# First two weight pairs of a hybrid HGRN2 and pooling block: four kinds of sums on GpSimd, masks sooner, splits and transposes in another order

## The chip, the core and the metric

The kernel runs on one core of one Trainium2 chip. The metric is the device time of one launch in microseconds (us). PE is TensorE (its matmuls), DVE is VectorE, ACT is ScalarE, POOL is GpSimd, SP is the queue that loads weights and tokens. L12 is line 12 of the kernel.

## The reference, cut to what matters

```
z = concat(16 meta tokens, x)                 # 1040 x 1024
h = rms_norm(z)                               # x * rsqrt(mean(x*x) + eps) * w
p = h @ w_in + b_in                           # 1024 x 8192: q, f, v, g_hg, u, g_pool, m_hg, m_pool
o = hgrn2_chunkwise(q, k, v, log f)           # 8 heads, chunks of 128 here
y_hg   = (rms_norm(o) * silu(g_hg)) @ w_down_hg
y_pool = (pool(u) @ pool_w * scale * silu(g_pool)) @ w_down_pool
z = z + (sigmoid(m_hg) * y_hg + sigmoid(m_pool) * y_pool) @ w_out
out = rms_norm(z)[16:]
```

All of it is float32. Nearly all of the time goes into the three large products with weights.

## The kernel before, in words

**Products.** Output columns are taken in 40 pairs of 128-column blocks. Each pair is a two by two block product with the 1024 tokens, made with seven smaller products instead of eight. `product(p, i)` is product i of pair p: weights `operand(p, i)` (128 x 512) against one of seven token operands, `R_B11, R_B21, R_V6, R_V5, R_V7, R_B22, R_V4` (i from 0 to 6, 128 x 2048 each). The weights of i = 2 to 5 are sums of the blocks of the raw weights: S2, S1, S3, S4. The token operands of i = 2, 3, 4, 6 are sums of blocks of h: V5 = B11 - B12, V6 = -(B22 + V5), V7 = B22 - B12, V4 = -(V6 + B21).

**Splits.** Each operand is split in a high part (reduced precision, made by ACT: `high(o)` for weights, `first_tile`, `second_tile`, `v5_high`, `v6_high`, `v7_high`, `v4_high` for tokens) and a low part, the exact operand less the high one (made by DVE: `low(o)`, `b22_low`, `v5_low` and so on). A product is 12 matmuls of 128 columns by 512: high by high, high by low and low by high for four blocks. Weight number o in `ORDER` uses slot o % 4 of a ring, so `high(o)` waits for product o - 4. In this order the first 14 products are (0,0) (0,1) (1,0) (1,1) (0,5) (1,5) (0,3) (1,3) (0,2) (1,2) (0,4) (1,4) (0,6) (1,6). They are called o0 to o13 below, and (2,0) is o14.

**Start.** x comes in eight tiles of 128 rows. For tile i ACT squares it (`square_x`), DVE makes the mean (`x_mean`), POOL the inverse root by pow (L556), DVE the row of h (`h_row`), PE turns it (`h_transposes`), and ACT and DVE copy and split it out of PSUM (`first_tile` and `first_low` for tiles 1 to 4, `second_tile` and `b22_low` for 5 to 8). o0 needs the low parts of tiles 1 to 4 (semaphore `h_lo` at 4), o4 all eight tiles, o6 `v5_lo`, o8 `v6_lo`, o10 `v7_lo`, o12 `v4_lo`.

**Orders.** Each engine runs a list that is written out by hand. DVE's list up to o14 holds, beside the splits, the weight sums of pairs 0 and 1 (`early_sums`, L1530 to L1534, and `early_third_sum`, L1539: eight of 128x512), the sums V5, V6, V7 and V4 (`v7_sum` L1472 and `v4_sum` L1505: two halves of 128x1024 each) and the sums of products that leave PSUM (`add_11`, `add_12`, `add_22`, `early_fifth`). POOL makes the inverse roots and then, when the last is made, the masks of the recurrence (memset L560, selects L563 and L579, casts L585 and L586), which DVE and ACT need before `prepare(0)`, just ahead of o14. The SP queue sends the weights of pair 2 when the low part of o12 is made (L475).

After o14 pairs follow one another, with the recurrence of the head before woven between products.

Of the kernel before, what the change touches and what calls it, by code (L numbers as in the profile page):

```python
# [12 lines left out]
P = 128  # L13
# [140 lines left out]
def hybrid_block(nc, x, meta, norm_w, wstream, pool_w, b_in, lb_logits, hg_norm_w, pool_scale, final_norm_w, out):  # L154
    names = ExitStack()
    with names:
# [7 lines left out]
            "hm_cleared", "hm_copied",  # L164
# [370 lines left out]
        def _(pool):  # L535
# [24 lines left out]
            steps.mark(pool.memset(mask1[:, :, :], 1.0))  # L560

            def keep(mask, base, channel, pattern):
# [3 lines left out]
            level0 = mask1[:, 0:2, :].rearrange("p a (b j) -> p (a b) j", j=2)  # L566
            odd = mask1[:, 3, :]
            halves = [(m, mask1[:, n, :].rearrange("p (b j) -> p b j", j=1 << m), lo, hi)
                      for m, n, lo, hi in ((1, 2, 0, 1), (2, 4, 0, 3), (3, 5, 4, 7), (3, 6, 0, 3), (4, 7, 0, 15))]
# [3 lines left out]
            for m, view, lo, _ in halves:  # L573
                keep(view, -lo, 1, [[-(2 << m), 64 >> m], [0, 1 << m]])
# [3 lines left out]
            for m, view, _, hi in halves:  # L578
                steps.mark(pool.affine_select(out=view, in_=view, compare_op=ALU.is_ge, fill=0.0, base=hi,  # L579
                                              pattern=[[2 << m, 64 >> m], [0, 1 << m]], channel_multiplier=-1))  # L580
            steps.settle()
            whole = mask1[:, 0:2, :].rearrange("p a t -> p (a t)")
            for g in range(GROUPS):
                rows = slice(g * GROUP, (g + 1) * GROUP)
                pool.tensor_copy(mask[rows, 0, :], whole[rows, rows])  # L585
                ins = pool.tensor_copy(mask[rows, 2:MASKS, 0:16], mask1[rows, 2:MASKS, g * 16:(g + 1) * 16])  # L586
            ins.then_inc(S["masks_spread"], 1)
# [76 lines left out]
        def _(act):  # L664
# [64 lines left out]
            def v4_high(n):  # L729
                c = slice(n * 2 * P, (n + 1) * 2 * P)  # L730
                act.wait_ge(S["v4_made"], n + 1)
                act.activation(r_hi[R_V4][:, :, c], r_lo_f[R_V4][:, :, c], ACT.Copy).then_inc(S["v4_hi"], 1)
# [222 lines left out]
            first_tile(4)  # L955
            square_x(6)
            high(1)
            square_x(7)
            act.wait_ge(S["lb_shifted"], 1)
            act.activation(lexp[:, :, :], lexp[:, :, :], ACT.Exp).then_inc(S["lb_exp"], 1)  # L960
            square_x(8)
            high(2)
# [6 lines left out]
            meta_copy(0, 0)  # L969
            second_tile(8)  # L970
            high(4)
            copy_first(1)
            v5_high()
            high(5)
            act.activation(o_ms[:, 0:1], minus_half[:, 0:1], ACT.Sigmoid)
            copy_early_fifth(0)
            high(6)
# [11 lines left out]
            meta_copy(0, 1)  # L989
            copy_second(1)  # L990
            v4_high(0)
            v4_high(1)
            high(11)
            act.wait_ge(S["lb_made"], 1)
            gates(0)
            high(12)
            high(13)
            prepare_copies(0)
            last_quarter(0)
            high(14)  # L1000
            high(15)
# [142 lines left out]
        def _(pe):  # L1144
# [92 lines left out]
            def product(p, i):  # L1237
                half(p, i, 0)
                half(p, i, 1)
# [184 lines left out]
        def _(dve):  # L1424
# [21 lines left out]
            def first_low(i):  # L1446
                c = slice((i - 1) * P, i * P)
                lower, upper = banks_of(i)
                dve.wait_ge(S["h_hi"], i)
                dve.tensor_tensor(r_lo[R_B11][:, :, c], lower, r_hi[R_B11][:, :, c].bitcast(F32), ALU.subtract)  # L1450
                dve.tensor_copy(b11_whole[:, :, c], lower)
# [14 lines left out]

            def v7_sum(n):

                dve.wait_ge(S["h_copied"], CHUNKS)
                dve.wait_ge(S["v6_made"], n + 1)  # L1470
                b22 = r_lo_f[R_V7][:, :, two(n)]
                dve.tensor_tensor(b22, b22, b12_whole[:, :, two(n)], ALU.subtract).then_inc(S["v7_made"], 1)  # L1472
# [30 lines left out]
            def v4_sum(n):  # L1503
                dve.wait_ge(S["v6_made"], n + 1)
                dve.scalar_tensor_tensor(r_lo_f[R_V4][:, :, two(n)], v6_whole[:, :, two(n)], -1.0, r_lo_f[R_V4][:, :, two(n)],  # L1505
                                         ALU.mult, ALU.subtract).then_inc(S["v4_made"], 1)

# [11 lines left out]
            def early_sums(p):  # L1519

                dve.wait_ge(raw_loaded[2 * p], 16)
                if p:
                    dve.wait_ge(S["early_loaded"], 16)
                    dve.wait_ge(S["h_row"], 8)
                else:
                    dve.wait_ge(raw_loaded[1], 16)
                a11, a12 = raw_half(p, 0, 0), raw_half(p, 0, 1)
                a21, a22 = (raw_early[:, 0:HALF], raw_early[:, HALF:D]) if p else (raw_half(0, 1, 0), raw_half(0, 1, 1))
                made, done = (sums_early if p else sums), S["sums_made"]
                dve.tensor_tensor(made[S1][:, :], a21, a22, ALU.add).then_inc(done, 1)  # L1530
                dve.wait_ge(done, sum_made(p, S1))
                dve.tensor_tensor(made[S2][:, :], made[S1][:, :], a11, ALU.add).then_inc(done, 1)
                dve.wait_ge(done, sum_made(p, S2))
                dve.tensor_tensor(made[S4][:, :], made[S2][:, :], a12, ALU.add).then_inc(done, 1)  # L1534

            def early_third_sum(p):

                a21 = raw_early[:, 0:HALF] if p else raw_half(0, 1, 0)
                dve.tensor_tensor((sums_early if p else sums)[S3][:, :], raw_half(p, 0, 0), a21, ALU.add) \  # L1539
                    .then_inc(S["sums_made"], 1)  # L1540

            def weight_sums(p):
# [4 lines left out]
                done = S["sums_made"]  # L1547
                dve.wait_ge(S["w_lo"], (POS[0, 4] if p == EARLY else POS[p - 1, 5]) + 1)
# [262 lines left out]
            first_low(1)  # L1811
            h_row(3)
            x_mean(4)
            first_low(2)
            h_row(4)
            x_mean(5)
            first_low(3)
            low(0)
            first_low(4)
            h_row(5)  # L1820
            x_mean(6)
            low(1)
            h_row(6)
            x_mean(7)
            low(2)
            h_row(7)
            x_mean(8)
# [4 lines left out]
            v5_sum(6)  # L1832
            add_11(0)
            low(3)
            early_sums(0)
            b22_low(7)
            v5_sum(7)
            b22_low(8)
            v5_sum(8)
            low(4)  # L1840
            early_sums(1)
            low(5)
            v5_low()
            add_11(1)
            low(6)
            dve.wait_ge(S["lb_exp"], 1)
# [7 lines left out]
            v6_sum(0)  # L1854
            v6_sum(1)
            low(7)
            v6_low(0)
            v6_low(1)
            early_fifth(0)
            low(8)  # L1860
            low(9)
            v7_sum(0)
            v7_sum(1)
            early_third_sum(0)
            early_third_sum(1)
            v7_low(0)
            v7_low(1)
            low(10)
            v4_sum(0)
            v4_sum(1)  # L1870
            add_12(0)
            low(11)
            add_22(0)
            v4_low(0)
            v4_low(1)
            low(12)
# [3 lines left out]
            add_22(1)  # L1880
            dve.wait_ge(S["masks_spread"], 1)
            prepare(0)
            low(14)
# [412 lines left out]
```

## Time and profile before

| | us |
|---|---|
| median of three runs (1080.66 to 1082.76) | 1081.52 |
| the profiled execution, its own time | 1081.81 |
| its span | 1079.9 |
| PE busy | 1040.1 (96%) |
| DVE busy | 778.2 (72%) |
| ACT busy | 490.4 (45%) |
| POOL busy | 97.7 (9%) |

The profiled execution took 1.9 us more than its span, for what lies around it. Busy times are shares of the span over very unlike stages: they say which engine is nearly full, not what a change in the first 80 us is worth. A start and a duration are read together: two instructions of one engine overlap by some 0.08 us, so that a DVE instruction of 0.68 us follows the one before at 0.60.

### The profile page before, as it was taken

The numbers are of one execution on the slowest core, as the hardware profiler recorded it, in microseconds if no ns is written. First come the engines' busy times: TensorE is split into PE (matmuls) and PEld (weight loads), VectorE is DVE, ScalarE is ACT, GpSimd is POOL, SyncE is SP. The second block draws the span as 40 slices with busy tenths as digits, with TensorE's granted clock in tenths as the row PEclk, the third lists the DMA queues.
The fourth block names the chain that finished last, engine by engine and source line by source line (L and its number), as shares of the span: only waits on it lengthen the run. The fifth ranks groups of instructions, "written<-read, shape, count | busy, mean of one in ns | idle before, by whom it ended". The sixth has DMA issues, their size and how long they took to land. (4 is left out here: it accounts for less than half of the span.)

```text
span 1079.9 us, 18838 instructions
## 1 busy us (share of the span) xinstructions
PE 1040.1 (96%) x7444; PEld 844.6 (78%) x7444; DVE 778.2 (72%) x1245; ACT 490.4 (45%) x841; POOL 97.7 (9%) x164
## 2 busy tenths in 40 slices
PE   7879999999999999999999999999999999999995
PEld 6657888888888888787888787788887787787884
DVE  7887686868686868686676767774569789978233
ACT  7664535353545454443353533344457246245122
POOL 2500010101010101010101010001110110000111
PEclk9999999999999999999999999999999999999998
DMA  6022020202020111122212121227332674555232
GB/s 257 1 81 77 21 80 21 80 20 80 21 70 31 61 39 60 41 69 79 80 57 89 58 89 50 82 74 301 117 108 98 236 271 156 175 177 175 69 121 103
DMA packets 36055, 104.61 MB, mean 97 GB/s; under 512 B 4576, under 2 KB 4576, under 8 KB 35968
## 3 DMA queue, kind: packets, MB, share of 16 engines
q1 hardware_dynamic: 22064, 65.61, 18.6%
q0 software_dynamic: 8240, 26.79, 6.7%
q10 hardware_dynamic: 5664, 11.02, 2.7%
q8 instruction: 59, 0.97, 0.4%
q14 instruction: 28, 0.23, 0.1%
HBM read 78.23 MB, written 25.17 MB: 96 GB/s over the span
## 5 line engine op out<-in xcount | busy, mean ns | idle before, releaser
L1149 PE MATMUL acc<-r_hi,w_hi 128*128 128x512 f32 x1112 | 448.0, 403 | 15.3 <-DVE w_lo L1516 5.3
L1149 PE MATMUL acc<-r_hi,w_lo 128*128 128x512 f32 x1112 | 434.2, 390 | 0.0
L1149 PE MATMUL acc<-r_lo,w_hi 128*128 128x512 f32 x1112 | 433.9, 390 | 0.0
L1149 PEld LDWEIGHTS acc<-r_hi,w_hi 128*128 128x128 f32 x1112 | 208.8, 188 | 70.4 <-issue 22.9
L1149 PEld LDWEIGHTS acc<-r_hi,w_lo 128*128 128x128 f32 x1112 | 208.7, 188 | 45.0
L1149 PEld LDWEIGHTS acc<-r_lo,w_hi 128*128 128x128 f32 x1112 | 209.1, 188 | 39.0
L678 ACT ACTIVATE w_hi<-sum 128x512 fp32r<-128x512 f32 x156 | 97.9, 628 | 150.5 <-DVE sum L1552 81.7
L1516 DVE TENSOR_TENSOR w_lo<-sum,w_hi 128x512 fp32r<-128x512 f32 x156 | 106.5, 686 | 59.8 <-ACT w_hi L678 59.5
L1516 DVE TENSOR_TENSOR w_lo<-raw,w_hi 128x512 fp32r<-128x512 f32 x120 | 82.1, 687 | 68.1 <-ACT w_hi L678 68.0
L678 ACT ACTIVATE w_hi<-raw 128x512 fp32r<-128x512 f32 x120 | 74.6, 624 | 26.2 <-PE acc L1149 26.2
L1149 PE MATMUL acc<-wo_hi,m_hi 128*128 128x512 f32 x128 | 49.9, 390 | 0.6 <-DVE wo_lo L2187 0.6
L1149 PE MATMUL acc<-wo_lo,m_hi 128*128 128x512 f32 x128 | 49.8, 389 | 0.0
L1149 PE MATMUL acc<-wo_hi,m_lo 128*128 128x512 f32 x128 | 49.8, 389 | 0.0
L762 ACT ACTIVATE second<-acc,bias 128x512 f32<-128x512 f32 x31 | 21.2, 685 | 61.0 <-PE acc L1149 60.9
L591 POOL TENSOR_TENSOR o_rs<-o_ms,minus_half 128x8 f32<-128x8 f32 x8 | 16.0, 2004 | 328.9 <-DVE o_ms L1769 328.9
L762 ACT ACTIVATE fifth<-acc,bias 128x512 f32<-128x512 f32 x31 | 21.3, 687 | 44.7 <-PE acc L1149 44.6
L762 ACT ACTIVATE first<-acc,bias 128x512 f32<-128x512 f32 x32 | 22.1, 690 | 38.0 <-PE acc L1149 37.9
L2051 DVE TENSOR_TENSOR r_lo<-stage,r_hi 128x2048 fp32r<-128x2048 f32 x14 | 32.0, 2285 | 1.9 <-ACT r_hi L1068 1.9
L1149 PEld LDWEIGHTS acc<-wo_hi,m_hi 128*128 128x128 f32 x128 | 24.0, 188 | 6.1 <-DVE wo_lo L2187 1.1
L1320 PE MATMUL miscs<-st,qx 128*128 128x128 f32 x128 | 25.6, 281 | 2.7 <-DVE st L1758 2.7
L1149 PEld LDWEIGHTS acc<-wo_hi,m_lo 128*128 128x128 f32 x128 | 24.0, 188 | 5.0
L1149 PEld LDWEIGHTS acc<-wo_lo,m_hi 128*128 128x128 f32 x128 | 24.0, 188 | 4.8
(287 smaller groups left out, 1380.5 us busy)
## 6 DMA issues: line engine op xcount, KB each, us to landing
raw<-in_wstream SPq DMA_DIRECT2D x88, 512.0 KB, 3.7
xin<-in_x SPq DMA_DIRECT2D x8, 512.0 KB, 6.1
a_spill<-gt POOLq DMA_DIRECT2D x16, 256.0 KB, 4.0
c_spill<-pg POOLq DMA_DIRECT2D x16, 256.0 KB, 2.7
stage<-a_spill ACTq DMA_DIRECT2D x4, 1024.0 KB, 12.4
smh_spill<-zq POOLq DMA_DIRECT2D x16, 256.0 KB, 2.6
gate_in<-smh_spill SPq DMA_DIRECT2D x16, 256.0 KB, 4.8
part_spill<-zq POOLq DMA_DIRECT2D x16, 256.0 KB, 4.7
```

Of the source, the lines that this page charges most:

```text
L591: pool.tensor_tensor(o_rs[:, :], o_ms[:, :], minus_half[:, 0:CHUNKS], ALU.pow).then_inc(S["o_rstd"], 1)
L678: act.activation(w_hi[o % RING][:, :], operand(o), ACT.Copy).then_inc(S["w_hi"], 1)
L762: return act.activation(dst, src, ACT.Identity, bias=b, scale=scale)
L1149: ins = pe.matmul(out_ap, a, b, start=first and n == 0, stop=final and n == 2, skip_group_check=partial)
L1320: pe.matmul(dst, qt[:, s], st[:, s], start=True, stop=False)
L1516: dve.tensor_tensor(w_lo[o % RING][:, :], operand(o), w_hi[o % RING][:, :].bitcast(F32), ALU.subtract) \
L2051: dve.tensor_tensor(r_lo[i][:, :, :], STAGED[i][:, :, :], r_hi[i][:, :, :].bitcast(F32), ALU.subtract) \
```

## The change

It touches the stage before o14 alone.

- POOL makes the eight weight sums of pairs 0 and 1 and the sums V7 and V4, which DVE made. V4 was one instruction of the form (in0 * -1) - in1; ACT now keeps B21 with its sign turned (`scale=-1.0`), so that V4 is a plain subtraction, -B21 - V6.
- POOL's mask instructions are put between the inverse roots, and the casts that spread the masks behind the weight sums.
- `first_low` is cut in three (`b11_low`, `b11_copy`, `b21_low`), and o0 waits only for the four low parts of B11.
- ACT, PE and DVE run their lists in another order: `high(4)` to `high(15)` sooner, transposes 5 to 8 half a product or more later, the tail of the lower bound's arithmetic (`lb`) later, V6 behind `v5_low` and ahead of `low(7)`.
- The third weight sums come before the masks are spread. `v4_high(n)` waits for `v6_low(n)` too, and `v7_sum` for the masks. `weight_sums(2)` waits for all eight early sums. The second pair's sums wait for all nine rows of h.

```diff
@@ gpsimd
-            for i in range(CHUNKS + 1):
+            def x_rstd(i):
                 rows = META if i == 0 else P
                 pool.wait_ge(S["x_mean"], i + 1)
                 pool.tensor_tensor(x_rs[...], x_ms[...], minus_half[...], ALU.pow).then_inc(S["x_rstd"], 1)
...
+            def early_sum(p, s):
...
+                if s == S1:
+                    pool.wait_ge(raw_loaded[2 * p], 16)
+                    if p:
+                        pool.wait_ge(S["early_loaded"], 16)
+                        pool.wait_ge(S["h_row"], CHUNKS + 1)
+                    else:
+                        pool.wait_ge(raw_loaded[1], 16)
+                    a, b = a21, a22
...
+                pool.tensor_tensor(made[s][:, :], a, b, ALU.add).then_inc(done, 1)
+            def v7_sum(n):
...
+                pool.wait_ge(S["h_copied"], CHUNKS)
+                pool.wait_ge(S["h_lo"], CHUNKS)
+                pool.wait_ge(S["v6_made"], n + 1)
+                pool.wait_ge(S["masks_spread"], 1)
+                b22 = r_lo_f[R_V7][:, :, c]
+                pool.tensor_tensor(b22, b22, b12_whole[:, :, c], ALU.subtract).then_inc(S["v7_made"], 1)
+            def v4_sum(n):
...
+                pool.wait_ge(S["v6_made"], n + 1)
+                b21 = r_lo_f[R_V4][:, :, c]
+                pool.tensor_tensor(b21, b21, v6_whole[:, :, c], ALU.subtract).then_inc(S["v4_made"], 1)
+            x_rstd(0)
+            steps.mark(pool.memset(mask1[:, :, :], 1.0))
+            (2 selects) x_rstd(1) (2) x_rstd(2) (2) x_rstd(3) (3) x_rstd(4) (2) x_rstd(5) (3) x_rstd(6)
+            early_sum(0, S1)
+            x_rstd(7)
+            early_sum(0, S2)
+            x_rstd(8)
+            early_sum(0, S4)
+            early_sum(1, S1)
+            early_sum(1, S2)
+            early_sum(1, S4)
+            early_sum(0, S3)
+            early_sum(1, S3)
+            spread_masks()
+            v7_sum(0)
+            v7_sum(1)
+            v4_sum(0)
+            v4_sum(1)
@@ scalar
-                act.activation(r_lo_f[R_V4][:, :, c], upper, ACT.Copy).then_inc(S["h_copied"], 1)
+                act.activation(r_lo_f[R_V4][:, :, c], upper, ACT.Copy, scale=-1.0).then_inc(S["h_copied"], 1)
...
             v6_high(0)
             v6_high(1)
-            high(7)
             high(8)
             high(9)
             v7_high(0)
+            high(10)
+            copy_second(0)
             v7_high(1)
-            copy_second(0)
-            high(10)
+            high(11)
@@ tensor
-                if p == 0 and i < 2:
+                if p == 0 and i == 0:
+                    pe.wait_ge(S["b11_lo"], 4)
+                elif p == 0 and i == 1:
                     pe.wait_ge(S["h_lo"], 4)
...
             product(0, 0)
+            half(0, 1, 0)
             h_transposes(5)
-            half(0, 1, 0)
+            half(0, 1, 1)
             h_transposes(6)
-            half(0, 1, 1)
+            half(1, 0, 0)
             h_transposes(7)
-            product(1, 0)
+            half(1, 0, 1)
             h_transposes(8)
@@ vector (the new order from tile 3 on)
+            h_row(4) x_mean(5) b11_low(3) low(0) b11_copy(3) b11_low(4) b21_low(3) b11_copy(4) b21_low(4) low(1)
+            h_row(5) x_mean(6) x_mean(7) h_row(6) x_mean(8) low(2) h_row(7) b22_low(5) v5_sum(5) h_row(8) b22_low(6)
+            add_11(0) low(3) v5_sum(6) b22_low(7) v5_sum(7) b22_low(8) low(4) v5_sum(8) low(5) add_11(1) low(6) v5_low()
+            v6_sum(0) v6_sum(1) low(7) v6_low(0) low(8) v6_low(1) early_fifth(0) low(9) (lb) v7_low(0) low(10) v7_low(1)
+            low(11) add_12(0) v4_low(0) add_22(0) low(12) v4_low(1) early_fifth(1) add_12(1) low(13) add_22(1) low(14)
+            prepare(0) low(15) weight_sums(2) low(16)
```

The lists of POOL's selects and of DVE are written in one line each here; in the kernel each call has its own line.

## Rows read from the trace of the kernel before

**Rows 1.** The page, parts 1 and 2: busy time; TensorE's granted clock in 40 slices.

```profile
PE 1040.1 (96%) x7444; PEld 844.6 (78%) x7444; DVE 778.2 (72%) x1245; ACT 490.4 (45%) x841; POOL 97.7 (9%) x164
PEclk9999999999999999999999999999999999999998
```

**Rows 2.** Busy time by stretch: start:end, length, PE, PEld, DVE, ACT, POOL, clock, DMA.

```profile
30.00:40.00 10.00, 9.02 (x50) 7.32 (x48) 9.93 (x15) 7.05 (x15) 9.79 (x17) 1.00 0.00 1
60.00:70.00 10.00, 7.10 (x32) 5.29 (x31) 8.96 (x11) 7.86 (x13) 0.00 (x0) 1.00 0.17 52
23.44:79.20 55.76, 46.24 (x237) 35.19 (x237) 47.25 (x64) 36.88 (x58) 15.15 (x26) 1.00 0.12 38
79.20:127.00 47.80, 47.59 (x530) 37.64 (x530) 34.92 (x70) 22.72 (x43) 1.16 (x2) 1.00 0.17 57
127.00:1065.00 938.00, 926.38 (x6547) 753.51 (x6548) 676.33 (x1078) 412.26 (x706) 73.57 (x113) 1.00 0.29 98
```

**Rows 3.** Timeline of PE: start, duration, instruction, idle before and its releaser.

```profile
20.02 1.50 PE L1335 MATMUL acc<-ident 128*128 128x128 f32 x12
23.44 0.47 PE L1149 MATMUL acc<-r_hi,w_hi 128*128 128x512 f32 x1 [1.91 <-DVE r_lo L1453]
...
40.46 0.47 PE L1149 MATMUL acc<-r_hi,w_hi 128*128 128x512 f32 x1 [1.44 <-DVE w_lo L1516]
...
43.07 0.39 PE L1149 MATMUL acc<-r_hi,w_lo 128*128 128x512 f32 x1
...
79.20 0.47 PE L1149 MATMUL acc<-r_hi,w_hi 128*128 128x512 f32 x1 [0.92 <-DVE w_lo L1516]
```

**Rows 4.** Timeline of DVE: splits of tile 4, sums that move, one that stays.

```profile
21.41 0.68 DVE L1450 TENSOR_TENSOR r_lo<-miscs,r_hi 128x512 fp32r<-128x512 f32 x1
22.01 0.68 DVE L1451 COPY b_whole<-miscs 128x512 f32<-128x512 f32 x1
22.61 0.68 DVE L1453 TENSOR_TENSOR r_lo<-miscs,r_hi 128x512 fp32r<-128x512 f32 x1
...
56.64 2.36 DVE L1472 TENSOR_TENSOR r_lo_f<-r_lo_f,b_whole 128x1024 f32<-128x1024 f32 x2
...
62.99 2.35 DVE L1505 SCALAR_TENSOR_TENSOR r_lo_f<-b_whole,r_lo_f 128x1024 f32<-128x1024 f32 x2
```

**Rows 5.** Groups of POOL's instructions by form: count, busy, mean ns.

```profile
L542 POOL TENSOR_SCALAR_AFFINE_SELECT stack<-stack 128x16 f32<-128x16 f32 x4 | 0.8, 199 | 0.7 <-POOL stack L539 0.2
L560 POOL MEMSET mask<- 128x512 f32 x1 | 0.5, 526 | 0.0
L545 POOL TENSOR_SCALAR_AFFINE_SELECT ident<-ident 128x128 f32<-128x128 f32 x1 | 0.3, 294 | 0.1
L537 POOL MEMSET ident<- 128x128 f32 x1 | 0.2, 205 | 0.3 <-POOLq L2286 0.3
```

**Rows 6.** Timeline of POOL: the masks.

```profile
30.74 5.79 POOL L563 TENSOR_SCALAR_AFFINE_SELECT mask<-mask 128x128 f32<-128x128 f32 x9
36.48 3.36 POOL L579 TENSOR_SCALAR_AFFINE_SELECT mask<-mask 128x64 f32<-128x64 f32 x5
```

**Rows 7.** Timeline of DVE before, and beside, POOL's selects.

```profile
28.21 1.29 DVE L1440 SCALAR_TENSOR_TENSOR hrow<-xin,x_rs,nw 128x1024 f32<-128x1024 f32 x1 [0.67 <-PE levels L1251]
...
30.96 1.47 DVE L1440 SCALAR_TENSOR_TENSOR hrow<-xin,x_rs,nw 128x1024 f32<-128x1024 f32 x1
...
32.36 0.72 DVE L1483 TENSOR_TENSOR r_lo<-r_lo_f,r_hi 128x512 fp32r<-128x512 f32 x1
...
35.61 0.82 DVE L1532 TENSOR_TENSOR sum<-sum,raw 128x512 f32<-128x512 f32 x1
...
39.64 0.72 DVE L1516 TENSOR_TENSOR w_lo<-sum,w_hi 128x512 fp32r<-128x512 f32 x1
```

**Rows 8.** Timelines of POOL and DVE around 139 us.

```profile
138.24 2.06 POOL L591 TENSOR_TENSOR o_rs<-o_ms,minus_half 128x8 f32<-128x8 f32 x1 [54.69 <-DVE o_ms L1769]
```

```profile
138.68 0.70 DVE L1689 TENSOR_TENSOR kt<-kt,fg 128x520 f32<-128x520 f32 x1
```

More of the change, by code:

```diff
@@ L557, in _, with runs @@
                                    ALU.pow).then_inc(S["x_rstd"], 1)
-            steps.mark(pool.memset(mask1[:, :, :], 1.0))
+            level0 = mask1[:, 0:2, :].rearrange("p a (b j) -> p (a b) j", j=2)
+            odd = mask1[:, 3, :]
+            def runs(m, n):
+                return mask1[:, n, :].rearrange("p (b j) -> p b j", j=1 << m)
             def keep(mask, base, channel, pattern):
@@ L564, in keep, with keep_from @@
                                               pattern=pattern, channel_multiplier=channel))
[L566 to L569, printed above, removed]
+            def keep_from(m, n, lo):
+                keep(runs(m, n), -lo, 1, [[-(2 << m), 64 >> m], [0, 1 << m]])
@@ new lines, in keep_to, with spread_masks @@
+            def keep_to(m, n, hi):
+                keep(runs(m, n), hi, -1, [[2 << m, 64 >> m], [0, 1 << m]])
+            def spread_masks():
+                steps.settle()
+                pool.wait_ge(S["sums_made"], 4 * EARLY)
+                whole = mask1[:, 0:2, :].rearrange("p a t -> p (a t)")
+                for g in range(GROUPS):
+                    rows = slice(g * GROUP, (g + 1) * GROUP)
+                    pool.tensor_copy(mask[rows, 0, :], whole[rows, rows])
+                    ins = pool.tensor_copy(mask[rows, 2:MASKS, 0:16], mask1[rows, 2:MASKS, g * 16:(g + 1) * 16])
+                ins.then_inc(S["masks_spread"], 1)
@@ new lines, in early_sum @@
+            def early_sum(p, s):
+                a11, a12 = raw_half(p, 0, 0), raw_half(p, 0, 1)
+                a21, a22 = (raw_early[:, 0:HALF], raw_early[:, HALF:D]) if p else (raw_half(0, 1, 0), raw_half(0, 1, 1))
+                made, done = (sums_early if p else sums), S["sums_made"]
+                if s == S1:
[6 more added lines that the diff above has]
+                    a, b = a21, a22
+                elif s == S2:
+                    pool.wait_ge(done, sum_made(p, S1))
+                    a, b = made[S1][:, :], a11
+                elif s == S4:
+                    pool.wait_ge(done, sum_made(p, S2))
+                    a, b = made[S2][:, :], a12
+                else:
+                    a, b = a11, a21
+                pool.tensor_tensor(made[s][:, :], a, b, ALU.add).then_inc(done, 1)
@@ L572, in _ @@
             keep(odd, -1, 1, [[-2, 64]])
-            for m, view, lo, _ in halves:
-                keep(view, -lo, 1, [[-(2 << m), 64 >> m], [0, 1 << m]])
+            x_rstd(1)
+            keep_from(1, 2, 0)
+            keep_from(2, 4, 0)
+            x_rstd(2)
+            keep_from(3, 5, 4)
+            keep_from(3, 6, 0)
+            x_rstd(3)
+            keep_from(4, 7, 0)
             steps.settle()
@@ L577, in _ @@
             keep(odd, 1, -1, [[2, 64]])
[L578 to L587, printed above, removed]
+            x_rstd(4)
+            keep_to(1, 2, 1)
+            keep_to(2, 4, 3)
+            x_rstd(5)
+            keep_to(3, 5, 7)
+            keep_to(3, 6, 3)
+            keep_to(4, 7, 15)
+            x_rstd(6)
+            early_sum(0, S1)
[13 more added lines that the diff above has]
+            v4_sum(1)
             def o_rstd(r):
@@ L969, in _ @@
             meta_copy(0, 0)
+            high(4)
             second_tile(8)
-            high(4)
+            high(5)
             copy_first(1)
+            high(6)
             v5_high()
-            high(5)
             act.activation(o_ms[:, 0:1], minus_half[:, 0:1], ACT.Sigmoid)
             copy_early_fifth(0)
-            high(6)
+            high(7)
             copy_early_fifth(1)
@@ L1517, in low @@
                     .then_inc(S["w_lo"], 1)
[L1519 to L1540, printed above, removed]
             def weight_sums(p):
@@ L1810, in _ @@
             x_mean(3)
-            first_low(1)
+            b11_low(1)
+            b11_copy(1)
+            b21_low(1)
             h_row(3)
             x_mean(4)
-            first_low(2)
+            b11_low(2)
+            b11_copy(2)
+            b21_low(2)
             h_row(4)
             x_mean(5)
-            first_low(3)
+            b11_low(3)
             low(0)
-            first_low(4)
+            b11_copy(3)
+            b11_low(4)
+            b21_low(3)
+            b11_copy(4)
+            b21_low(4)
+            low(1)
             h_row(5)
             x_mean(6)
-            low(1)
+            x_mean(7)
             h_row(6)
-            x_mean(7)
+            x_mean(8)
             low(2)
             h_row(7)
-            x_mean(8)
             b22_low(5)
@@ L1838, in _ @@
             b22_low(8)
+            low(4)
             v5_sum(8)
-            low(4)
-            early_sums(1)
             low(5)
-            v5_low()
             add_11(1)
             low(6)
+            v5_low()
+            v6_sum(0)
+            v6_sum(1)
+            low(7)
+            v6_low(0)
+            low(8)
+            v6_low(1)
+            early_fifth(0)
+            low(9)
             dve.wait_ge(S["lb_exp"], 1)
@@ L1853, in _ @@
             dve.tensor_scalar(one_minus_lb[:, :], lb[:, :], -1.0, 1.0, ALU.mult, ALU.add).then_inc(S["lb_made"], 1)
[L1854 to L1865, printed above, removed]
             v7_low(0)
+            low(10)
             v7_low(1)
-            low(10)
-            v4_sum(0)
-            v4_sum(1)
+            low(11)
             add_12(0)
-            low(11)
+            v4_low(0)
             add_22(0)
-            v4_low(0)
+            low(12)
             v4_low(1)
-            low(12)
             early_fifth(1)
@@ L1880, in _ @@
             add_22(1)
+            low(14)
             dve.wait_ge(S["masks_spread"], 1)
             prepare(0)
-            low(14)
             low(15)
```

48 lines of the change are left out of this document (24 added, 24 removed).

## The prediction

> **What bounds the kernel now.** I read the page first. PE is busy 96% of the span, and its clock is the higher of its two levels, 2.4 GHz, in every slice but the last [rows 1]. So a gain has to be found where PE is not busy. The busy times by stretch say where that is. From 79.20 to 127 us PE idles 0.2 of 47.8 us, and up to 1065 us it idles 11.6 of 938 us, spread thinly. From 23.44 us, when o0 starts, to 79.20 us, when o14 starts, it idles 55.76 - 46.24 = 9.5 us, 17% [rows 2]. Behind o14 PE's own work sets the pace, so a time at which o14 starts sooner or later comes through to the end one for one. The start of o14 is the number to predict.
>
> The timeline of PE names the waits. o0 begins 1.9 us after the last warming matmul, released by DVE's low part of tile 4 (L1453). Nine breaks follow, the first ahead of o4 (1.44 us) and the last ahead of o14 (0.92 us), most of them released by `low` (L1516) on DVE [rows 3]. PE's ends are modelled. The twelve starts of o4 lie 0.24 us apart, but its last matmul is shown as 0.39 long, so each break is some 0.16 longer from start to start. Nine of these make 1.5 us, and the true idle time is 11.0 us. DVE itself is busy 9.93 of 10 us from 30 to 40, and 8.96 from 60 to 70 [rows 2]. It is the engine behind these waits.
>
> **The change part by part.**
>
> o0's wait. It now waits for `b11_low(4)`. Before, DVE did B11 low, the copy and B21 low of tile 4 one after another, 21.41 to 23.29 [rows 4]. In the new list `b11_low(4)` starts when ACT has made the high part, 20.8, and ends at 21.5, as PE's warming matmuls do. o0 starts at 21.5: 1.9 us gained, if nothing later takes it back.
>
> What leaves DVE. Eight sums at 0.60 us are 4.8, V7 and V4 at 2.28 each from start to next start [rows 4] are 4.6. Together 9.4 us.
>
> With DVE never hindered, I walked the four lists, each instruction starting when its engine is free and its semaphores stand, with the spacings of these timelines (0.60 for 512 columns on DVE, 1.14 for 1024, 0.49 and 1.05 on ACT, 1.41 for half a product). The same walk over the old lists gives o14 at 78.6, against 79.20 in the trace. The new lists give o4 37.0, o8 49.0, o10 55.2, o12 60.9 and o14 68.0. Breaks of 0.4 and 0.5 us are left, and 1.4 ahead of o14, where ACT's `high(14)` stands behind the four gate instructions. That is 10.6 us sooner: 1.9 + 11.0 - 2.3. The order of splits and transposes has no price of its own in it. The transposes that slip cost nothing because o1 to o3 stand between them, and the later `lb` nothing because ACT's gates come 11 us after it; were either cover gone, 0.8 us for a transposition or 0.7 us for `lb` would show. Pair 2's weights leave SP when the low part of o12 stands, which is sooner by as much, so they keep their distance. New waits: behind `v7_sum` on POOL stands `v4_sum`, and for it ACT's `v4_high`. Behind ACT's `copy_second(0)` (o8's end) stands `v7_high(1)`, and DVE's `v7_low(1)` waits for that 2 us in the walk, under cover of o8 and o9.
>
> What comes to POOL. No row shows a plain sum there. A memset of 512 columns took 0.526 and one of 128 took 0.205; a select of 128 columns took 0.294 and of 16 took 0.199 [rows 5]. Both give 0.84 us per thousand columns over a floor near 0.19. A sum reads two operands; if they go one after the other a 512-column sum takes 0.19 + 0.87 = 1.06 and a 1024-column one 1.93. Twelve sums are 8 x 1.06 + 4 x 1.93 = 16.2 us. From the seventh inverse root (25.7) POOL has time: unhindered, V7 begins at 43 and V4's second half at 49, ready for o10 (55) and o12 (61). The inverse roots for tiles 7 and 8 now stand behind a sum each. That sets `h_row(7)` back by at most 1.1 us, covered by o1 and o2.
>
> What the two do to each other. This decides. While POOL ran its masks, 14 selects took 9.1 us, 0.65 each, for a kind that takes some 0.25 alone [rows 5, 6]: each waited for the DVE instruction in hand. DVE lost little, but it lost something at each one. An `h_row` took 1.47 instead of 1.29, a sum 0.82, eight others, from 32.36 to 39.64, 0.72 instead of 0.685 [rows 7]. All these read two operands from SBUF. Together DVE lost 0.60 us while the selects read 2 x 128 + 12 x 64 = 1024 columns: 0.60 us per thousand. The moved sums read 8 x 1024 + 4 x 2048 = 16384 columns. At that rate they hold DVE for 9.8 us. Of DVE's 30.7 us from `h_row(7)` to `low(13)` only eight instructions (4.8 us: `add_11`, `add_12`, `add_22`, `early_fifth`, one operand from PSUM) are of another kind, so I let 0.8 of it fall on the path: 7.8 us.
>
> The Trainium skill (SBUF — State Buffer, "Who interferes with whom") has the same as a rule: a VectorE instruction with two SBUF inputs and a GpSimd instruction that reads SBUF use one read interface, and the later one is blocked until the first has finished. The rows bear out the waiting on both sides. By the duration that GPSIMD Engine Reference, "Performance versus the Vector engine", states for a sum of 2048 columns (4497 ns), an estimate for the twelve sums is 17.2 us of hold, and the sum below would be 1084.7 instead.
>
> **The sum.** 10.6 - 7.8 = 2.8 us sooner. The profiled execution took 1081.81, 1.9 more than its span, and would take 1079.0; the median of runs lies 0.3 lower: 1078.7.
>
> Bounds of the hold. Below: nothing, 10.6 sooner, 1070.9. A 520-column product of DVE beside a POOL pow of 2.06 us took 0.70, no longer than elsewhere [rows 8], so a POOL instruction doesn't hold DVE by its mere presence. Above, from the 128-column selects alone: 0.18 us lost beside one [rows 7] is 1.4 us per thousand columns, and 23 us of hold, 18 on the path, 7.8 slower. I take 0.60 because it comes from all 14, and halfway between the two rates, 1.0, for the far end of the range: 16.4 x 0.8 = 13.1, 2.5 slower, 1084.0; some 1.5 us of error of the walk on top, 1085.5. The walk shows why this end is near. With POOL's V7 and V4 sums each holding DVE 1.7 us, they fall between `v6_sum(1)`, `low(7)`, `v6_low(0)`, `low(8)` and `v6_low(1)`, and o8 waits nearly 6 us.
>
> **Rivals.**
>
> *A. DVE is held for the whole of each POOL sum.* The twelve sums last 16.2 us; 13.0 on the path: 2.4 slower, 1083.9. From 1082.0, if the fixed 0.19 us of each is free (13.9 us of hold), to 1085.5, if a sum is slower than 1.06 us. It turns the change into a loss from a hold of 13.3 us on, 0.81 per thousand columns. For it: the loss beside 128-column selects. Against it: the loss beside those of 64 columns, 0.035, less than 64 columns take at POOL's pace (0.054).
>
> *B. DVE is hardly held.* POOL's reads fit into gaps, or run ahead. 1071 to 1074.5. For it: the pow row and the small mean loss. Against it: all selects were delayed by DVE, so the two do exclude each other.
>
> *C. POOL becomes the bound.* If a sum of 1024 columns takes 4 us, V4 is complete at 43 + 16 = 59 and its two high and two low parts at 63, and o12 waits 2 us beyond the rest: 1073 when nothing is held, 1081 with the hold of my sum. It needs a rate four times that of the rows.
>
> **Chances.** Forecast case (1075 to 1081.2) 0.39; A 0.36; B 0.19; C and others 0.06. A reaches from 1081.2 to 1086. By what a measurement of this kernel can tell from no change, 0.2% or 2.2 us, faster means below 1079.4: B, two thirds of the forecast case, 0.47 in all. Within 0.2%: the rest of the forecast case and a quarter of A, 0.23. Slower, over 1083.7: 0.30. The range 1070.9 to 1085.5 leaves 0.12 out, mostly above. The likeliest case alone spans 1075 to 1081.2.
>
> **What the next profile would show.** o0 at 21.5 (right if within 0.3). POOL's sums at 1.06 and 1.93, plus up to 0.6 of waiting. DVE's two-operand instructions between 26 and 58 lengthened: by 0.6 for each 512-column sum and 1.2 for each 1024-column one in my case, 1.1 or more in A, none in B. o4 near 40.7, o8 between 53 and 57, o14 near 76. If o14 starts before 71 or after 79, the hold was mis-sized. If it starts as foretold and the end does not follow, the pace behind o14 is not PE's own.

## The result, and the profile after

| | before | after |
|---|---|---|
| median us | 1081.57 (7 runs, 1080.66 to 1082.76) | 1086.08 (7 runs, 1085.23 to 1086.36) |
| the profile's span, us | 1079.9 | 1084.3 |
| start of o0 / o4 / o14, us | 23.44 / 40.46 / 79.20 | 21.30 / 43.90 / 84.49 |

The ratio of after to before is 1.0039, with a 95% interval of 1.0028 to 1.005: the kernel became 4.5 us slower, where 2.8 us sooner was forecast. It arises ahead of o14, which starts 5.3 us later.

The page of the kernel after, parts 1 and 2 (beside [rows 1]): DVE has 6.3 us more busy time, although twelve of its instructions went away, and POOL 24.1 us more.

```profile
PE 1044.0 (96%) x7444; PEld 848.5 (78%) x7444; DVE 784.5 (72%) x1233; ACT 489.6 (45%) x841; POOL 121.8 (11%) x176
PEclk9889999999999999999999999999999999999998
```

The busy times by stretch of the kernel after (beside [rows 2]; start:end, length, PE, PEld, DVE, ACT, POOL, clock, DMA):

```profile
40.00:50.00 10.00, 6.11 (x16) 4.92 (x17) 9.83 (x10) 5.12 (x7) 6.29 (x10) 0.66 0.17 56
...
60.00:70.00 10.00, 6.63 (x17) 5.22 (x18) 6.77 (x9) 1.13 (x2) 2.14 (x1) 0.66 0.00 0
...
21.30:84.49 63.19, 50.69 (x236) 39.37 (x237) 56.71 (x58) 37.98 (x62) 31.36 (x23) 0.89 0.11 35
84.49:1069.00 984.51, 973.34 (x7075) 790.88 (x7076) 709.51 (x1141) 434.71 (x749) 74.54 (x115) 1.00 0.28 96
```

From o0 to o14 PE now needs 63.19 us for what took 55.76, and idles 12.5 of them instead of 9.5. PE's busy time rose too, 50.69 against 46.24, and in two of the stretches its clock is 0.66. The timeline of PE in the kernel after (beside [rows 3]) says where:

```profile
21.30 0.47 PE L1227 MATMUL acc<-r_hi,w_hi 128*128 128x512 f32 x1 [0.17 <-DVE r_lo L1531]
...
36.58 0.47 PE L1227 MATMUL acc<-r_hi,w_hi 128*128 128x512 f32 x1 [1.28 <-DVE w_lo L1593]
...
43.90 0.77 PE L1227 MATMUL acc<-r_hi,w_hi 128*128 128x512 f32 x1 [4.31 <-DVE w_lo L1593]
44.46 0.63 PE L1227 MATMUL acc<-r_lo,w_hi 128*128 128x512 f32 x1
44.88 0.63 PE L1227 MATMUL acc<-r_hi,w_lo 128*128 128x512 f32 x1
...
63.37 0.77 PE L1227 MATMUL acc<-r_hi,w_hi 128*128 128x512 f32 x1 [4.81 <-DVE r_lo L1571]
...
84.49 0.50 PE L1227 MATMUL acc<-r_hi,w_hi 128*128 128x512 f32 x1 [1.15 <-ACT vt L840]
```

o0 starts 2.1 us sooner. The nine breaks became five, 12.5 us in all, two of them large: 4.31 us ahead of o4 and 4.81 ahead of o8, both released by DVE. Behind each the matmuls start 0.43 us apart instead of 0.23: the granted clock is at the lower of its two levels, 1.2 GHz, from 42.3 to 49.1 and from 62.7 to 69.5 us. The timelines of DVE and of POOL in the kernel after, first DVE (beside [rows 4, 7]):

```profile
25.47 2.31 DVE L1521 SCALAR_TENSOR_TENSOR hrow<-xin,x_rs,nw 128x1024 f32<-128x1024 f32 x1 [0.61 <-POOL x_rs L556]
...
31.18 1.77 DVE L1550 TENSOR_TENSOR r_lo_f<-b_whole 128x512 f32<-128x512 f32 x1
...
34.68 0.68 DVE L1656 TENSOR_TENSOR fg<-acc,first 128x512 f32<-128x512 f32 x1
35.28 1.16 DVE L1593 TENSOR_TENSOR w_lo<-raw,w_hi 128x512 fp32r<-128x512 f32 x1
36.36 1.78 DVE L1550 TENSOR_TENSOR r_lo_f<-b_whole 128x512 f32<-128x512 f32 x1
...
50.92 2.90 DVE L1593 TENSOR_TENSOR w_lo<-sum_early,w_hi 128x512 fp32r<-128x512 f32 x1
53.99 3.17 DVE L1571 TENSOR_TENSOR r_lo<-b_whole,r_hi 128x1024 fp32r<-128x1024 f32 x1 [0.17 <-ACT r_hi L795]
57.09 2.86 DVE L1593 TENSOR_TENSOR w_lo<-sum,w_hi 128x512 fp32r<-128x512 f32 x1
59.87 3.36 DVE L1571 TENSOR_TENSOR r_lo<-b_whole,r_hi 128x1024 fp32r<-128x1024 f32 x1
...
70.54 1.23 DVE L1582 TENSOR_TENSOR r_lo<-r_lo_f,r_hi 128x1024 fp32r<-128x1024 f32 x1 [3.66 <-ACT r_hi L804]
```

```profile
25.40 1.29 POOL L607 TENSOR_TENSOR sum<-raw 128x512 f32<-128x512 f32 x1
26.65 1.53 POOL L556 TENSOR_TENSOR x_rs<-x_ms,minus_half 128x1 f32<-128x1 f32 x1
...
34.33 1.56 POOL L607 TENSOR_TENSOR sum_early<-raw_early 128x512 f32<-128x512 f32 x1 [1.92 <-DVE hrow L1521]
...
50.10 5.98 POOL L617 TENSOR_TENSOR r_lo_f<-r_lo_f,b_whole 128x1024 f32<-128x1024 f32 x2 [3.54 <-DVE b_whole L1560]
56.04 6.10 POOL L624 TENSOR_TENSOR r_lo_f<-r_lo_f,b_whole 128x1024 f32<-128x1024 f32 x2
```

POOL's first sum starts at 25.40 and lasts 1.29. The row of h that starts at 25.47 takes 2.31 instead of 1.28: DVE lost 1.03 us. A 512-column difference beside a sum takes 1.77 instead of 0.68. `add_11` at 34.68, with one operand in PSUM, takes its usual 0.68 beside the sum of 34.33, and only the `low` behind it is lengthened, by 0.48, for the rest of that sum. Beside V7 and V4 four DVE instructions take 2.90, 3.17, 2.86 and 3.36 where 0.69 and 1.22 are usual. Added over all twelve sums, DVE was held for 7.95 us by the eight of 512 columns (1.07 for a full one) and for 8.47 us by the four of 1024 (2.1 each): 16.4 us for 16384 columns read, 1.00 us per thousand. What left DVE was 9.4 us. The trade costs DVE 7.0 us. V7 and V4 do worse than their own balance, 8.5 us of hold against 4.6 that left: the hold falls wholly ahead of o8, the saving behind it, where DVE stands 3.66 us for the second high part of V7. ACT makes that behind its copy of o8's result, so it can't come sooner than o8 lets it.

### The profile page after: what moved, and what is told of

Same layout as the page of the kernel before. It is cut to its first block and busy times, and to the rows that moved or that the text cites. A ratio compares the mean times of both kernels' runs of the same rounds, so it can differ in the third digit from the quotient of the medians.

```text
span 1084.3 us, 18844 instructions
## 1 busy us (share of the span) xinstructions
PE 1044.0 (96%) x7444; PEld 848.5 (78%) x7444; DVE 784.5 (72%) x1233; ACT 489.6 (45%) x841; POOL 121.8 (11%) x176
## 5 line engine op out<-in xcount | busy, mean ns | idle before, releaser
L1593 DVE TENSOR_TENSOR w_lo<-sum,w_hi 128x512 fp32r<-128x512 f32 x156 | 108.8, 701 | 60.0 <-ACT w_hi L755 59.7
L704 POOL DMA_DIRECT2D c_spill<-pg x16 | 8.6, 539 | 181.8 <-DVE pg L2054 181.3
```

The lines of the kernel that those rows point to most:

```text
L704: pool.dma_start(c_dram[2 * g + k // 2, k % 2], pg[:, k // 2, (k % 2) * HALF:(k % 2 + 1) * HALF]).then_inc(c_stored[k], 16)
L1593: dve.tensor_tensor(w_lo[o % RING][:, :], operand(o), w_hi[o % RING][:, :].bitcast(F32), ALU.subtract) \
```

## The experiments

Three theories stood after this. **Hold**: DVE stands still while a sum of POOL reads, if DVE's instruction has both operands in SBUF, and this net 7 us is most of the loss. **Order**: the new lists themselves are bad. **Clock**: the lower clock behind the two waits is most of the loss. A fourth, that DVE or PE simply waits for POOL's results, is out by the rows above: V4's second half is ready at 62.1 us, and no break stands ahead of o10 or o12. Every kernel but those said otherwise is the kernel after with the edit shown. Ratios and differences are to the kernel before, which ran again beside each group of them (medians 1082.08, 1082.30 and 1082.10 us).

### All sums on DVE again, everything else of the change kept

```diff
-            early_sum(0, S1)      # POOL: all eight, v7_sum, v4_sum
...
+            early_sums(0)         # DVE: ahead of v5_sum(6)
+            early_sums(1)         # ahead of low(4)
+            v7_sum(0) v7_sum(1) early_third_sum(0) early_third_sum(1) v4_sum(0) v4_sum(1)
```

The masks are then spread behind the last inverse root, without waiting for the sums.

> The changed kernel with its eight weight sums and the sums V7 and V4 put back on DVE; the early start of o0, the masks between the inverse roots and all other orders stay. Theory 1 (DVE is held for some 1.07 us by each 512-column sum of POOL and 2.1 us by each 1024-column one, and this hold makes the loss): nothing holds DVE, o4 near 39, o8 near 53, o14 near 75.5, time 1077.7 (1076 to 1079.5). Theory 2 (the new order of splits, transposes and high parts costs by itself): 1081.5 or more, with waits at the same places as in the changed kernel. Theory 3 (the waits are cheap, the fall of TensorE's clock behind the two long ones makes most of the loss): the clock stays at the higher level, and the time is that of the changed kernel less 5.2 us, 1080.9.

Measured: 1077.09 us (1076.07 to 1077.28), ratio 0.9954, interval 0.994 to 0.9967. This is 5.0 us faster than before and 9 faster than after. The timeline of PE with all sums on DVE:

```profile
38.63 0.47 PE L1215 MATMUL acc<-r_hi,w_hi 128*128 128x512 f32 x1 [2.08 <-DVE w_lo L1581]
...
60.62 0.47 PE L1215 MATMUL acc<-r_hi,w_hi 128*128 128x512 f32 x1 [2.06 <-DVE r_lo L1570]
```

o4 starts 5.3 us sooner than after, with twelve sums more on DVE's list. So the order isn't what costs: the theory of the order fell, and the new order, with the early start and the masks between the inverse roots, is itself a gain. The second wait shown, 2.06 us, stands ahead of o10.

### Only the weight sums, only V7 and V4, only the early start

```diff
 (only the weight sums on POOL: V7 and V4 back)
-            v7_sum(0) v7_sum(1) v4_sum(0) v4_sum(1)          # POOL
+            v7_sum(0) v7_sum(1) ... v4_sum(0) v4_sum(1)      # DVE
 (only V7 and V4 on POOL: weight sums back)
-            early_sum(0, S1) ... early_sum(1, S3)            # POOL
+            early_sums(0) ... early_sums(1) ... early_third_sum(0) early_third_sum(1)   # DVE
 (kernel before with the early start alone)
-                if p == 0 and i < 2:
+                if p == 0 and i == 0:
+                    pe.wait_ge(S["b11_lo"], 4)
...
-            first_low(3)
+            b11_low(3)
...
-            first_low(4)
+            b11_low(4)
+            rest_low(3)
+            rest_low(4)
```

> The changed kernel with V7 and V4 back on DVE; POOL makes the eight weight sums only. Theory 1: DVE loses some 8 us up to o4, which starts near 44 as in the changed kernel; then no more is lost, no long wait ahead of o8, o14 near 77 to 79, time 1079.7 to 1082 (the higher figure if the clock falls behind the wait ahead of o4 and nothing hides it). Theory 2: over 1084. Theory 3: one fall of the clock instead of two, 1083.5.

> The changed kernel with the weight sums back on DVE; POOL makes V7 and V4 only. Theory 1: o4 near 39; DVE loses 8.5 us around v6_low, o8 near 61 with a wait over 4 us ahead of it, the clock falls there, o14 near 80 to 83, time 1082.8 to 1085.7. This part of the change costs more than the weight sums do. Theory 2: 1084 or more, with no more lost at v6_low than elsewhere. Theory 3: one fall of the clock, 1083.5.

> The kernel before with one part of the change: the low part of B11 of tile 4 is made ahead of the other four splits of tiles 3 and 4, and o0 waits for it alone. o0 starts at 21.3 to 21.5 instead of 23.44. If DVE's list sets the time from o4 on, as I think, the rest comes no sooner: wait ahead of o4 grows from 1.4 to 3, o14 near 79, time 1081.5 (1080.5 to 1082). If PE's own work mattered there, 1079.6.

| kernel | median us | ratio, interval | o4 | o14 |
|---|---|---|---|---|
| only the weight sums on POOL | 1080.00 | 0.9984, 0.9976 to 0.9993 | 44.06 | 78.46 |
| only V7 and V4 on POOL | 1084.25 | 1.0021, 1.0012 to 1.003 | 38.55 | 81.53 |
| before, early start alone | 1081.66 | 0.9995, 0.9986 to 1.0004 | 39.83 | 78.58 |

The timeline of PE with only the weight sums on POOL has the wait ahead of o4, while o8 (the second row) starts without one:

```profile
44.06 0.77 PE L1223 MATMUL acc<-r_hi,w_hi 128*128 128x512 f32 x1 [4.33 <-DVE w_lo L1589]
...
58.65 0.39 PE L1223 MATMUL acc<-r_hi,w_hi 128*128 128x512 f32 x1
```

With only V7 and V4 on POOL it is the other way round: o8 waits 6.38 us, and a `low` beside a sum of V7 takes 2.88 us. Timelines of PE and DVE:

```profile
60.97 0.77 PE L1219 MATMUL acc<-r_hi,w_hi 128*128 128x512 f32 x1 [6.38 <-DVE r_lo L1563]
```

```profile
48.58 2.88 DVE L1585 TENSOR_TENSOR w_lo<-sum_early,w_hi 128x512 fp32r<-128x512 f32 x1
```

Each group of sums makes its own wait. Against all sums on DVE (1077.09) the weight sums cost 2.9 us, near the 3.1 by which they hold DVE longer than they save it. V7 and V4 cost 7.2, where that balance is 3.9: their saving comes behind o8, and the clock is at 1.2 GHz from 58.6 to 65.4 us; what each of the two adds was not told apart. Together that is 10.1, where the whole change costs 9.0. The early start alone brings o0 2.6 us forward (23.44 to 20.84) and o14 by 0.6; its 0.4 us at the end can't be told from nothing. PE waits part of it away ahead of o4 (2.46 instead of 1.44 us) and loses part to the clock, which is at 1.2 GHz from 40.8 to 44.2 us. DVE's work is the limit, not the time at which PE begins.

### The kernel after, with PE kept at work in the two waits

```diff
+                if (p, i) in ((0, 5), (0, 2)):
+                    pe.wait_ge(S["h_copied"], CHUNKS - 1)
+                    for _ in range(18 if i == 5 else 20):
+                        pe.matmul(small[:, 0:P], ident[:, :], ident[:, :], start=True, stop=True)
```

> The changed kernel with warming matmuls (128 columns, into a PSUM bank that is free then) on PE: 18 ahead of o4 and 20 ahead of o8, the two waits of 4.3 and 4.8 us behind which the clock was at its lower level for 5.6 and 6.2 us. DVE and POOL are left alone. If the hold of DVE makes most of the loss and the clock the rest, o4 and o8 start as late as before (43.9, 63.4), the products behind o8 take 2.76 us each again, and 2 to 3 us come back: 1083.5 (1082.5 to 1084.5). The first slow stretch gives nothing back, since o8 waits for DVE anyway. If the clock were most of the loss, both stretches would come back: 1080.9.

The extra matmuls write scratch in PSUM that nobody reads. Measured: 1084.53 us (1083.37 to 1087.31), ratio 1.0024, interval 1.0015 to 1.0032, in the timeline of PE:

```profile
39.70 4.18 PE L1446 MATMUL levels<-ident 128*128 128x128 f32 x36
44.20 0.47 PE L1227 MATMUL acc<-r_hi,w_hi 128*128 128x512 f32 x1 [0.32 <-DVE w_lo L1597]
...
63.66 0.47 PE L1227 MATMUL acc<-r_hi,w_hi 128*128 128x512 f32 x1 [1.92 <-DVE r_lo L1575]
```

o4 and o8 start when they did (0.3 later), because DVE sets them, but their matmuls run at the higher level. 1.0039 to 1.0024 is 1.6 us, uncertain by about 1.5, as the two intervals just overlap; 2 to 3 were expected. In the profiled executions o14 starts 2.3 us sooner (82.22) and the span is 1.7 shorter. The clock is a minor part of the loss, and its theory as the main cause fell.

The same trick on the kernel with all sums on DVE (8 matmuls ahead of o4 and o10), where the clock was low from 61.2 to 64.6 us:

> The kernel with all sums on DVE and eight warming matmuls ahead of o4 and of o10, where PE waited 2.1 us each and behind the second of which the clock was at its lower level from 61.4 to 64.6 us. If the clock there costs what its matmuls lost (3.2 us at half rate), 1.5 us come back: 1075.5. If the fall is chance from run to run, the time stays within 0.5 us of 1077.1.

Measured 1077.14 us (1077.07 to 1078.31), ratio 0.9956, interval 0.9944 to 0.9969: no change from 1077.09. In its timeline of PE the time saved is waited away two products later, ahead of o12:

```profile
67.60 0.47 PE L1215 MATMUL acc<-r_hi,w_hi 128*128 128x512 f32 x1 [0.97 <-DVE r_lo L1579]
```

The lower clock cost nothing here because DVE was behind anyway; the expected gain missed for that reason.

### Three kinds of work on POOL beside the same DVE

The kernel before, with four memsets, four copies and four sums of 128x512 added to POOL behind the masks, all on scratch. ACT waits for them before it uses that scratch, so the kernel's time is not compared; its rows are.

```diff
+            left, right = vv[:, 0:HALF], vv[:, HALF:SEQ]
+            for kind in range(3):
+                for n in range(4):
+                    (0) pool.memset((left, right)[n % 2], 0.0)
+                    (1) pool.tensor_copy(left, right)
+                    (2) pool.tensor_tensor(left, left, right, ALU.add)
```

> The kernel before, and behind its masks POOL runs 4 memsets, 4 copies and 4 sums of 128x512 on scratch, one after another, while DVE works through v5_low, V6 and its splits (43 to 60 us). A reading of the hold by kind. If DVE is held for as long as POOL reads, a memset holds nothing, a copy about 0.45 us, a sum 1.07 us. If it is held for the whole instruction, a memset 0.5, a copy 0.6, a sum 1.28. If the hold has to do with POOL's writes, a memset holds DVE too. The time is not the question; some 5 us slower.

Measured: 1086.36 us, one run. The timelines of POOL and DVE; the last of the four copies, and each of the two V6 sums (L1493), are shown by themselves:

```profile
44.13 2.28 POOL L594 MEMSET vv<- 128x512 f32 x4
46.48 3.48 POOL L596 COPY vv<-vv 128x512 f32<-128x512 f32 x4
49.32 0.63 POOL L596 COPY vv<-vv 128x512 f32<-128x512 f32 x1
50.04 7.37 POOL L598 TENSOR_TENSOR vv<-vv 128x512 f32<-128x512 f32 x4
```

```profile
44.63 2.28 DVE L1509 TENSOR_TENSOR r_lo<-r_lo_f,r_hi 128x2048 fp32r<-128x2048 f32 x1
46.83 0.68 DVE L1615 TENSOR_TENSOR qx<-acc,first 128x512 f32<-128x512 f32 x1
47.44 0.68 DVE L1531 TENSOR_TENSOR w_lo<-sum,w_hi 128x512 fp32r<-128x512 f32 x1
48.03 0.57 DVE L1862 TENSOR_TENSOR lmax<-lexp 128x8 f32<-128x8 f32 x1
...
49.40 1.63 DVE L1493 SCALAR_TENSOR_TENSOR b_whole<-r_lo_f,r_lo_f 128x1024 f32<-128x1024 f32 x1
50.95 2.31 DVE L1493 SCALAR_TENSOR_TENSOR b_whole<-r_lo_f,r_lo_f 128x1024 f32<-128x1024 f32 x1
54.91 1.38 DVE L1531 TENSOR_TENSOR w_lo<-sum_early,w_hi 128x512 fp32r<-128x512 f32 x1 [1.64 <-ACT w_hi L691]
56.21 3.42 DVE L1504 TENSOR_TENSOR r_lo<-b_whole,r_hi 128x1024 fp32r<-128x1024 f32 x2
```

Four memsets, which read nothing, ran beside a DVE instruction with two operands in SBUF without lengthening it (2.28, its usual time). A copy, which reads 512 columns, held `lmax`, 8 columns of the lower bound, for 0.42 us (0.57 instead of 0.15), and another held the first V6 sum for 0.42 (1.63 instead of 1.21). A sum, which reads 1024, held the second V6 sum for 1.10 (2.31), and one of the two V6 low parts for 1.06 (3.42 for two that take 2.36). The `low` at 54.91, which began while a sum was under way, was held for the rest of it, 0.69. So what holds DVE is how much POOL reads, and not that POOL is busy.

### All sums on DVE, with DVE's and ACT's lists reordered

```diff
 (ACT)  second_tile(5) behind high(3), high(6) and v6_high(0) sooner, v4_high(0) behind v7_high(0), v7_high(1) ahead of copy_second(0)
 (DVE)  the weight sums one at a time between splits instead of three in a row; low(2) behind add_11(0);
        early_third_sum(0) ahead of low(8), v4_sum ahead of v7_sum, v7_low(0) and v7_low(1) ahead of lb, early_fifth(0) later
```

> The kernel with all sums on DVE (1077.09 in its run), with the lists of DVE and ACT put in an order in which each sum and split comes just ahead of its user: S1 of pair 0 between the rows of h, second_tile(8) ahead of high(4), V7's high parts ahead of copy_second. DVE's work is the same, its idle time less. A walk over the lists gives o14 3.9 us sooner than for the kernel with all sums on DVE: 1073.5 (1072 to 1076). If DVE's plain amount of work sets the time there, nothing comes of it: 1077.

Measured: 1072.88 us (1072.45 to 1073.77), ratio 0.9917, interval 0.9903 to 0.993: 9 us faster than before, the best version here. Its timeline of PE (o4 and o10), and its busy times from 60 to 70 us:

```profile
37.75 0.47 PE L1215 MATMUL acc<-r_hi,w_hi 128*128 128x512 f32 x1 [0.40 <-DVE w_lo L1581]
...
59.17 0.47 PE L1215 MATMUL acc<-r_hi,w_hi 128*128 128x512 f32 x1 [1.39 <-DVE r_lo L1570]
```

```profile
60.00:70.00 10.00, 10.00 (x46) 8.02 (x45) 10.00 (x15) 8.56 (x12) 0.00 (x0) 1.00 0.56 191
```

PE and DVE are both full there, with POOL idle.

### Two sums given back to POOL, in two places

From that best version, S1 and S2 of pair 0 go to POOL again: once at 19 us, where DVE's splits have an operand in PSUM, and once beside the rows of h, whose operands are in SBUF.

```diff
             x_rstd(5)
+            early_sum(0, S1)      # first kernel
+            early_sum(0, S2)
...
             x_rstd(6)
+            early_sum(0, S1)      # second kernel
             x_rstd(7)
+            early_sum(0, S2)
```

> The version with all sums on VectorE and its lists reordered, with the first two weight sums of pair 0 given back to GpSimd, at once behind the reciprocal root of the sixth row tile, so from about 19 us on, where VectorE does splits whose second operand is in PSUM (such a split was not lengthened in the two traces where a sum of GpSimd ran beside it). Theory of the hold (VectorE stands while GpSimd reads, if VectorE has two operands in SBUF): if the raw weights have landed by 22 us both sums lie beside PSUM splits and cost nothing, VectorE's list is 1.2 us shorter, and the time is 1071.7 to 1072.9. If the weights come later, or the reciprocal roots of the next tiles are put back by the sums, the rows of h come later and it is 1073 to 1075. Rival (any work that leaves VectorE helps by its own length, wherever GpSimd does it): about 1072, the same as its neighbour with the sums under the rows of h.

> The same two sums on GpSimd, but one behind the reciprocal root of the seventh and one behind that of the eighth row tile, so beside the rows of h, which have two operands in SBUF. Theory of the hold: each sum lengthens a row of h from 1.28 to about 2.3 us and saves 0.6 us later, so these rows' transposes and the product behind them come 1 to 2 us later and the list is 0.9 us longer in all; 1073.0 to 1074.9. Rival (any work that leaves VectorE helps by its own length): about 1072, like its neighbour.

Measured: 1073.33 us (1072.37 to 1073.56), ratio 0.9919 (0.9905 to 0.9933), for the first place, and 1075.95 us (1074.0 to 1076.55), ratio 0.994 (0.9928 to 0.9953), for the second. The same two sums cost 2.6 us more in the second place. Timelines of POOL and DVE in the first place:

```profile
19.33 1.73 POOL L607 TENSOR_TENSOR sum<-raw 128x512 f32<-128x512 f32 x1
21.13 1.30 POOL L607 TENSOR_TENSOR sum<-sum,raw 128x512 f32<-128x512 f32 x1
```

```profile
19.24 0.68 DVE L1583 TENSOR_TENSOR w_lo<-raw,w_hi 128x512 fp32r<-128x512 f32 x1
...
21.09 0.68 DVE L1532 TENSOR_TENSOR r_lo<-levels,r_hi 128x512 fp32r<-128x512 f32 x1
```

and of DVE and PE in the second:

```profile
25.84 2.30 DVE L1511 SCALAR_TENSOR_TENSOR hrow<-xin,x_rs,nw 128x1024 f32<-128x1024 f32 x1 [0.61 <-POOL x_rs L556]
```

```profile
32.13 0.50 PE L1217 MATMUL acc<-r_hi,w_hi 128*128 128x512 f32 x1 [2.16 <-DVE w_lo L1583]
...
33.46 0.63 PE L1217 MATMUL acc<-r_lo,w_hi 128*128 128x512 f32 x1
```

In the first place the sum of 21.13 and the split of 21.09 ran side by side, each at its own length; the sum of 19.33 waited 0.45 us for a `low` with two SBUF operands that had begun before it. The hold theory is right about this. But its gain missed: DVE's list is 1.2 us shorter, but o10 still waits 1.39 us for the same split (`v7_low`), and the time is that of the version without (1072.88) within what can be told. DVE gaps appear instead, one of 0.51 ahead of a row of h. In the second place both rows of h took 2.30, o2 waited 2.16 us instead of 0.56, and behind it, from 32.8 to 36.2 us, the clock was at 1.2 GHz. The median lies 1.1 us above the top of what the theory gave; the theory left the clock out, which may account for it; that was not tried by itself. The rival, that any work off DVE helps equally, is out.

## Why the prediction was wrong

**The start of o0.** Foretold 21.5, found 21.30. Right. But the 1.9 us that stand in the sum are no gain by themselves: alone the early start brought 0.4 us, which can't be told from nothing, since DVE's list didn't get shorter.

**What leaves DVE**, 9.4 us, was right. **With DVE unhindered, 10.6 us sooner.** No kernel can take the sums off DVE for nothing, so this was not tested by itself. The sentence that the new order of splits has no price of its own was wrong, in the good direction: order, masks and early start together brought 5.0 us with all sums still on DVE, and the early start is at most 0.4 of it. Which of the other pieces brings the rest was not tried singly.

**POOL's sums.** Foretold 1.06 us for 512 columns, found 1.29. A sum of 1024 never ran alone; two with DVE's instructions between took 5.98. Inverse roots between the sums took 1.53 us instead of 0.55, as they stood behind a row of h. "Covered by o1 and o2" was wrong for these: 0.95 us of waiting for the transposes of tile 8 and 1.28 ahead of o3.

**The hold: the step that failed.** The prediction took 0.60 us per thousand columns, the mean over 14 selects, and 9.8 us in all. It is 1.00, and 16.4 us. Two things were too small in it. POOL goes through a sum more slowly than through a select: 1.29 us less the floor of 0.19 is 1.07 per thousand columns read, not 0.84 (an estimate with the floor of [rows 5]). And DVE is held for all of that, not for 0.7 of it. The mean was drawn down by selects of 64 columns, beside which DVE lost 0.035 us where their reading takes 0.054 [rows 7]; why these short ones show less was not tried. The 128-column selects gave 1.4 and erred the other way. The far end's rate, 1.0, is what happened. Rival A, with a 0.36 chance, was the case that came, nearly by its own signs: DVE's two-operand instructions 1.03 to 1.10 us longer beside a 512-column sum, and the long wait ahead of o8 that the walk gave for such holds (4.81 us here, nearly 6 there). Its turning point, a hold of 13.3 us, was passed. That its 16.2 us come so near to 16.4 is partly luck: it had DVE held for the whole of sums of 1.06 us, and the hold is 1.07 of 1.29. Rival C, POOL as the bound, did not come: no product waited for V7 or V4.

The Trainium skill (SBUF — State Buffer, "Who interferes with whom") says that of a VectorE instruction with two SBUF inputs and a GpSimd instruction that reads SBUF the later is blocked until the first has finished. The trace agrees that they exclude each other, but not that it is for the whole instruction: 1.03 to 1.10 us were lost beside 1.29, and the pow of 2.06 us that was under way in [rows 8] held nothing. The memsets, which read nothing, are outside that rule and held nothing. The estimate by the figure of the Trainium skill's GPSIMD Engine Reference, "Performance versus the Vector engine", 17.2 us of hold and 1084.7, was nearer than the rate taken from the rows.

**The share on the path, 0.8.** With 16.4 us of hold, 0.8 of it is 13.1, and 10.6 - 13.1 is 2.5 us slower. No run measured the 0.8, and a single share is too coarse: it depends on what the held instructions stand ahead of, as V7 and V4 show.

**The omitted term: the clock.** The prediction read the clock as high throughout and said nothing of what two waits of over 4 us would do to it. It cost 1.6 us, within the error given, by the kernel that kept PE at work. 10.6 - 13.1 - 1.6 = -4.1 against -4.5 measured; that this closes so well is partly luck, as neither 10.6 nor 0.8 was measured. What was measured, against the kernel with all sums on DVE, is 9.0 us of loss, for 7.0 net on DVE and 1.6 of clock. Without the clock the time would have been some 1084.5, inside the range to 1085.5: the hold made the forecast miss its direction, the clock carried it past the range.

**Where it ends.** From o14 on the end followed one for one within a microsecond (o14 5.3 later, span 4.4): right. o4 at 40.7, o8 between 53 and 57 and o14 at 76 were foretold with the hold too small; they came at 43.90, 63.37 and 84.49. The prediction's own sign of a mis-sized hold, o14 after 79, was there.

## What to carry to other kernels

Count a two-input sum that goes to GpSimd as its whole reading time taken from VectorE, wherever VectorE works on two SBUF operands: here 1.07 us for a 0.60 us sum. Beside VectorE instructions with a PSUM operand it was free, and even there it brought nothing measurable, while the next long wait stayed. Ask too where the hold and the saving fall: a hold ahead of a product and a saving behind it don't cancel. When a price is a mean over short instructions, ask what a long one would do, and put the rate of the longest rows inside the range as a case of its own. Order the lists first: with the same 9.4 us of sums left on VectorE and interleaved one at a time, the new lists gave 9 us.

## What the runs showed of the hardware

- DVE with two SBUF operands beside POOL: a 128x512 memset held it 0, a copy 0.42, a sum 1.03 to 1.10, a 128x1024 sum 1.95 to 2.2 us. With one operand in PSUM (`add_11`, the splits at 21 us): 0.
- The other way round POOL waited too: 0.45 us for a `low` in hand, and an inverse root of one column took 1.53 us instead of 0.55.
- TensorE's granted clock went to 1.2 GHz in or behind waits of 2.06 us (all sums on DVE, ahead of o10), 2.16 (second place), 2.46 (early start alone), 4.31 and 4.81 (after), 4.33 (only the weight sums) and 6.38 (only V7 and V4), for 3.4 us behind the first three and 6.8 behind the others, and matmuls then started 0.43 us apart instead of 0.23. Behind the 1.44 us of [rows 3] it did not. With all sums on DVE it stayed up behind the 2.08 us ahead of o4: the length of the wait alone doesn't decide, and what does was not tried.
